# The rows that an expert block computes, cut from three steps of rank to four (128, 112, 104, then 96 from rank 22)

## The reference, cut to what matters

```python
grp = top-1 of 4 groups; two best of the 8 experts in that group     # 32 experts, 1536*2 = 3072 rows
for each expert e, for its own rows xb:                              # xb: tokens that chose e
    h = silu(xb @ w1[e]) * (xb @ w3[e])      # w1, w3: 1024 x 512
    y = h @ w2[e]                            # w2: 512 x 1024
out[token] += gate * y
```

```
144 130 120 117 | 109 108 107 107 107 101 100 100 99 98 | 97 96 96 95 94 92 91 90 | 90 88 88 85 84 78 78 68 59 56
```

## Time and profile before

| | us |
|---|---|
| median of the runs | 1596.06 |
| lowest, highest | 1595.56, 1600.31 |
| the profiled execution | 1602.02 |
| its span, first to last instruction | 1600.4 |
| TensorE busy in the span | 1491.9 (93%) |
| VectorE, ScalarE, GpSimd busy | 524.3, 394.0, 185.2 |
| mean granted TensorE clock | 0.969 of full speed |

### The profile page before, as it was taken

One profiled execution on the slowest core, in us unless ns is written; L12 is line 12 of the kernel. 1 busy time (PEld: TensorE's weight loads), 2 busy tenths in 40 slices (PEclk: granted clock), 3 DMA queues, 4 the chain that ended last, 5 costly groups with the idle time before them and its releaser, 6 DMA issues.

```text
span 1600.4 us, 32656 instructions
## 1 busy us (share of the span) xinstructions
PE 1491.9 (93%) x13884; PEld 948.3 (59%) x13884; DVE 524.3 (33%) x1085; ACT 394.0 (25%) x577; POOL 185.2 (12%) x244
## 2 busy tenths in 40 slices
PE   7999999999999997999893899999999999999990
PEld 3444445555555554545451778777777777777750
DVE  3860035535536545454458201111111111111114
ACT  4120044454446434222440100000000000000004
POOL 2011000110010010011101111111111111111110
PEclk9999999999999998999995899999999999999995
DMA  6132132233123314435582949999999999999968
GB/s 231 40 105 86 66 138 73 73 106 110 63 98 102 118 68 142 160 138 204 201 288 101 361 148 320 360 359 355 357 356 353 357 367 361 367 364 363 365 199 328
DMA packets 75254, 350.07 MB, mean 219 GB/s; under 512 B 9704, under 2 KB 22504, under 8 KB 62752
## 3 DMA queue, kind: packets, MB, share of 16 engines
q1 hardware_dynamic: 56624, 288.31, 48.7%
q0 software_dynamic: 17968, 58.97, 12.4%
q10 hardware_dynamic: 576, 1.59, 0.3%
HBM read 285.69 MB, written 63.14 MB: 218 GB/s over the span
## 4 chain that ended last, share of the span: by engine, by line
PE 52%; DVE 3%; DMA 2%; ACT 2%; issue 2%; DVEq 0%; SPq 0%; POOLq 0%; ACTq 0%
PE bank L1947 24%; PE bank L1965 13%; PE bank L1762 7%; PE bank L1835 2%; PE bank L1920 2%; DMA wup<-w 1%; PE bank L1853 1%; ACT junk L1077 1%; PE bank L1847 1%; PE bank L1705 0%; PE bank L1980 0%; DVE wide L1359 0%; DMA x_dram<-mid,sidx 0%; DVE early L1505 0%; PE bank L1714 0%
## 5 line engine op out<-in xcount | busy, mean ns | idle before, releaser
L1613 PE MATMUL bank<-wide,mid 128*128 128x512 f32 x960 | 422.0, 594 | 1.1 <-issue 1.1
L1947 PEld LDWEIGHTS bank<-xgT,wup 128*64 128x64 f32 (+1 forms) x7680 | 396.2, 141 | 29.6 <-issue 23.7
L1947 PE MATMUL bank<-xgT,wup 128*64 128x104 f32 (+3 forms) x7680 | 403.1, 258 | 5.9 <-issue 3.4
L1613 PEld LDWEIGHTS bank<-wide,mid 128*128 128x128 f32 x960 | 179.4, 190 | 213.5 <-issue 212.8
L1965 PE MATMUL bank<-wide,hidT 128*128 128x512 f32 x512 | 225.6, 593 | 1.6 <-DVE mid L1546 1.6
L1965 PEld LDWEIGHTS bank<-wide,hidT 128*128 128x128 f32 x512 | 94.8, 190 | 109.5 <-issue 107.1
L1537 DVE TENSOR_TENSOR hidT<-sil,bank 128x512 f32<-128x512 f32 x30 | 20.6, 688 | 348.8 <-PE bank L1947 298.2
L1762 PE MATMUL bank<-early,mid 128*128 128x512 f32 x288 | 129.2, 603 | 2.5 <-issue 2.5
L804 POOL DMA_INDIRECT x_dram<-mid,sidx x32 | 50.2, 1568 | 535.1 <-DVE gidx L1523 484.3
L1060 ACT ACTIVATE sil<-bank 128x512 f32<-128x512 f32 x30 | 17.9, 597 | 381.5 <-PE bank L1947 381.5
L1546 DVE TENSOR_SCALAR mid<-bank,gate_of 128x512 f32<-128x512 f32 x64 | 48.0, 751 | 192.8 <-PE bank L1965 192.8
(11 more groups left out here) (250 smaller groups left out, 1254.9 us busy)
## 6 DMA issues: line engine op xcount, KB each, us to landing
wup<-w SPq DMA_DIRECT2D x64, 2048.0 KB, 16.1
wide<-w SPq DMA_DIRECT2D x32, 2048.0 KB, 10.1
u_dram<-ustage POOLq DMA_DIRECT2D x60, 256.0 KB, 2.3
rin<-u_dram SPq DMA_DIRECT2D x60, 256.0 KB, 4.4
mid<-w_in SPq DMA_DIRECT2D x23, 512.0 KB, 3.6
wide<-x_t SPq DMA_DIRECT2D x12, 512.0 KB, 11.5
mix_dram<-mixst POOLq DMA_DIRECT2D x24, 256.0 KB, 2.7
mid<-x_all SPq DMA_DIRECT2D x12, 512.0 KB, 5.5
```

What stands on the lines that cost most here:

```text
L1613: last = pe.matmul(PROJ[u % 3][:, :], wsec[:, slot, k, :], nT[:, k, g * GT:(g + 1) * GT], start=(k == 0), stop=(k == KT - 1))
L1947: last = pe.matmul(target[c0:c0 + wide_tile, at:at + rows], weights[:, s, k, f * P + c0:f * P + c0 + wide_tile], xgT[:, k, 0:rows], start= ...
```

## The change

The number of rows drops in one step more: 112 from rank 4, 104 from rank 14 (16 before), 96 from rank 22 (new). `CAPACITY` feeds everything that has a width: the loops of `blocks_loop` become 4 to 14, 14 to 22, 22 to 30 and 30 to 32, and the matmuls, transposes, gathers and adds take their rows from it. The VectorE lines that work out `cap` from `rank` are written for any number of steps: four instructions of 32 columns in place of three. The bound on overflow blocks is worked out more tightly; it is 30 before and after, so no tensor of the routing changes its width.

```diff
-CAPACITY = ((0, 128), (4, 112), (16, 104))
+CAPACITY = ((0, 128), (4, 112), (14, 104), (22, 96))
+FEWER = 8
 MAIN_BLOCKS = NE
 SIX = 6
-MAX_OVER = -(-(2 * T // (CAPACITY[-1][1] + 1)) // SIX) * SIX
+LEAST, LESS = CAPACITY[-1][1] + 1, CAPACITY[-2][1] + 1
+LATE = min(NE, 2 * T // LEAST) - CAPACITY[-1][0]
+MAX_OVER = -(-(LATE + (2 * T - LATE * LEAST) // LESS) // SIX) * SIX
...
-        cap_step = sb(blockwise, "cap_step", [P, len(CAPACITY) - 1, NE])
+        cap_step = sb(blockwise, "cap_step", [P, NE])
...
-            for i, (first, rows) in enumerate(CAPACITY[1:]):
-                link(dve.tensor_scalar(cap_step[:, i, :], rank[:, :], float(first), float(rows - CAPACITY[i][1]),
-                                       ALU.is_ge, ALU.mult))
-            link(dve.scalar_tensor_tensor(out=cap[:, :], in0=cap_step[:, 0, :], scalar=float(CAPACITY[0][1]),
-                                          in1=cap_step[:, 1, :], op0=ALU.add, op1=ALU.add))
+            steps = [(first, (CAPACITY[i][1] - rows) // FEWER) for i, (first, rows) in enumerate(CAPACITY[1:])]
+            assert all(n == 1 for _, n in steps[1:])
+            link(dve.tensor_scalar(cap_step[:, :], rank[:, :], float(steps[0][0]), float(steps[0][1]),
+                                   ALU.is_ge, ALU.mult))
+            for first, _ in steps[1:]:
+                link(dve.scalar_tensor_tensor(out=cap_step[:, :], in0=rank[:, :], scalar=float(first),
+                                              in1=cap_step[:, :], op0=ALU.is_ge, op1=ALU.add))
+            link(dve.tensor_scalar(cap[:, :], cap_step[:, :], -float(FEWER), float(CAPACITY[0][1]),
+                                   ALU.mult, ALU.add))
```

## The result

The changed kernel took 1602.73 us (median of 18 runs, 1599.02 to 1607.37) against 1599.17 us (18 runs, 1595.56 to 1600.83) for the kernel before: a ratio of 1.0021, 95% interval 1.0014 to 1.0029. That is 0.2% slower, where 0.5% faster was forecast, and it lies outside the range. A difference this small is under the 0.3% that the prediction called telling; with 18 runs each, its interval excludes no change all the same. Of the 14.5 us between 1588.2 and 1602.73, 3.1 are the kernel before itself: the forecast started from 1596.06, the median of three runs, and the median of 18 is 1599.17. The profiled execution took 1604.1 us, with a span of 1602.3.

The account below looks back on a forecast made before the run. TensorE was taken to bind to block 15 or so, the stream of weights and rows from 17; 7.2 (stream) + 0.9 (last step) - 0.2 (`cap` chain) = 7.9 us off 1596.06 gave 1588.2 us, range 1583.5 to 1593.5.

Parts of the forecast that it names:

- The reading of the bound: Expert stage: TensorE binds to block 15 or so, the stream of weights and rows from 17 on.
- no floor from weight loads: Up products: 96 rows take 10.7 us; rival that weight loads hold them at 11.56 us: 1589.1 us, chance 0.02.
- The landing of w1: Weight loads: w1 still lands 18 to 19 us after issue; near 15 would mean TensorE decides.
- The waits for weights: Between steps of the expert stage: waits for w1 begin about block 16.
- The stream's price for a 96-row step: Gather and add both with 96 rows: the stream needs 19.24 us a step, 19.94 less 0.70.
- Its two parts: Stream saving per 96-row step: 0.27 us for eight rows less moved, 0.43 us for leaving 104-row transfers.
- the awkwardness of 104: Indirect gathers and adds: 104 rows make more small packets and slow the stream, taken at 0.43 us a step.
- The gain of 7.2 us between the starts of step 14 and 31: Expert stage, stream decides: 328.0 us in place of 335.2, a gain of 7.2 us.
- The last step: Behind the last w3 only TensorE counts: block 31 gives 0.9 us.
- the one on the loops: One more boundary between loops of different width, on four engines: cost between 0 and 1.3 us, taken as 0.
- The slower rival I named: An expert over its new cap runs a 33rd block of 128 rows, 21.9 us: 1610.1 us, chance 0.03.
- the first weight wait: Expert stage: waits for w1 were to begin about block 16, the 4 us to spare being used up earlier.

Follow-up runs that it names:

- the kernel with even transfers: Kernel before, TensorE at 104 rows from block 16 as before, but gathers and adds of these blocks moving 112 rows: 1596.51 us, ratio 0.9976 to before.
- the one with the moved code: Changed kernel with 128 long-fulfilled waits put in TensorE's queue ahead of the wait for the picks: 1598.41 us, ratio 0.9984 to before.
- the early product: Changed kernel with block 31's down product ahead of the overflow loops where no overflow block is in use: 1589.92 us, ratio 0.9937 to before.
- the one jump: Changed kernel with one more condition around TensorE's overflow loops, left in one jump instead of five rounds: 1591.85 us, ratio 0.9940 to before.
- the run with one loop more: Kernel before with its loop of blocks 16 to 30 cut in two at block 22, widths as before: 1606.04 us, ratio 1.0038.
- the kernel with four widths: Kernel before with 112 rows, 104 from rank 10, 96 from 16, block 31's down product ahead of the overflow loops, even transfers: 1583.97 us, ratio 0.9892.

## Why the prediction was wrong

**What held.** The reading of the bound held. Up products with 96 rows were forecast at 10.7 us and are 10.71 to 10.78: no floor from weight loads. The landing of w1 stays at a median of 17.9 us from step 23 on, and no overflow block ran. The waits for weights came later than forecast, not about block 16 but ahead of block 20 (start, us, what, and in brackets the wait before it):

```profile
1311.12 11.63 PE L1954 MATMUL bank<-xgT,wup 128*64 128x104 f32 x256 [0.77 <-DMA wup<-w]
```

The kernel before, too, has its first wait between steps ahead of block 19 (the 1.02 us at 1293.54 in the earlier trace rows). The stream's price for a 96-row step was put at 19.24 us; eight steps from 23 to 30 took 152.3, 19.0 each. Its two parts held too. A step's packets under 512 B went back from 123 to about 80; the DMA view of step 26 of the changed kernel, without its last 0.4 us, has 77:

```profile
DMA packets 631, 6.72 MB, mean 361 GB/s; under 512 B 77, under 2 KB 77, under 8 KB 269
```

GpSimd's issue of the add went from 1616 ns to 1439, in the view of its line (min/median/max):

```profile
L807 POOL DMA_INDIRECT x_dram<-mid,sidx x7: 1439/1439/1457, 1390.5 to 1505.4; - x7
```

That the awkwardness of 104 costs the stream, taken at 0.43 us a step, is shown by the kernel with even transfers: its step of 19.32 us has 0.33 us less than the 19.65 that went by before, with 8 rows more to move at 0.27 us. That is at least 0.6 us, since TensorE sets the step there: the same side and a little larger. The rule of the Trainium skill that was cited for it, 13 engines for 104 rows ("DMA: Bandwidth & Descriptors"), agrees with this in its consequence, with an estimate of 0.73 us a step in the prediction; how the rows lie on the engines no trace shows.

**The gain of 7.2 us between the starts of step 14 and 31** measured 5.5. The missing 1.7 is about what TensorE waited, with no transfer named, in the first pass through the new loops:

```profile
1212.36 5.32 PE bank L1954 x114
1217.68 0.16 issue
1217.83 5.93 PE bank L1954 x128
1223.76 0.64 issue
1224.40 0.93 PE bank L1954 x14
...
1359.65 1.08 issue
```

These stand inside an up product and not at the start of a matrix, so they aren't waits for w1 or w3, and a q8 packet comes 1 to 3 us ahead of each (in the half microseconds from 1215.0, 1222.0 and 1358.0). Nine of the twelve profiles have a wait in the second block of a loop's first pass with just 14 matmuls of the up products to go, of 0.1 to 1.3 us; the one with the moved code has none there. That they are instruction waits is argued from that, not tried by itself. With the early product, where the waits in step 15 come to 0.2 us, the same stretch took 1519.66 - 1191.75 = 327.9 us; forecast were 328.0.

**The last step** was to bring 0.9 us by block 31. Its up product was 0.85 us shorter, but the transposes lost 1.0, so the term came out at nothing.

**The step that failed** is the one on the loops: "There is one boundary between loops of different width more ... Bounds 0 and 1.3 us; I take 0". I looked for the cost of a longer text at the boundary that was added. It came up behind the last main block, at the overflow loops, which the change doesn't touch: 8.5 us in the profile, 13 us between the medians of the changed kernel and of the one with the early product, 2 of which the kernel before has as well. The bound of 1.3 us was taken from the boundaries between main loops; the nearest row for this jump was the 1.6 us between the last two `down` products in the kernel before, and I gave it no term. With 8.5 us for it, from the profile, the sum comes out 0.6 us slower, and with the 11 us that the one jump brought back 3.1; measured were 3.6 between the medians. The fetch of instructions has a line in the page's DMA part, and I gave it neither a term nor a rival. The slower rival I named, an overflow block, didn't come.

Stated as sizes: without the jump the forecast holds. The kernel with the early product is 10.1 us under before by its ratio; less the 2 us that this edit is worth by itself, the change brings some 8 us, against 7.9 forecast. That the two agree so closely is in part luck, since the term of the last step and the time of the first weight wait were off.

**What stays open.** Why in some executions of one and the same program the wait is there and in others not (two bundles in the run with one loop more) wasn't settled. That the wait is a fetch of instructions rests on what the edits of the program's text did and on the times of the packets; no row names it. Nor was TensorE's exact count of blocks of code ahead of each jump worked out.

## What to carry to other kernels

Count the program's text as a resource: each further loop body moves everything behind it, and a loop whose conditions are all false isn't free when it jumps over its body once a round. Leave unlikely code in one jump and put the work of the usual case ahead of it; here that turned a change from 0.2% slower to 0.6% faster. And try to round the rows of indirect transfers to a multiple that measures well (96 or 112 here, not 104), even where less is computed; it took 4 us off the kernel before and nothing clear off the changed kernel, whose narrow blocks have even transfers already.

## What the runs showed of the hardware that I had not expected

- TensorE stood still for 8.3 us in the changed kernel with all data there, between two products with five rounds of a loop of false conditions between them; with one condition around the loop it didn't stand still at all, and the kernel was 11 us faster.
- The same program text moved by 128 instructions was 4 us faster by the medians.
- The still stretch cost the clock as well: 0.60 and then 0.50 of full speed granted, and 16 matmuls of 512 columns took 8.92 us instead of 7.14. In the kernel with four widths the clock was at 0.50 after only 2.3 us without a matmul, and an up product took 12.44 us instead of 10.71.
- Gathers and adds of 104 rows gave about 45 packets under 512 B more in a step than those of 112, and slowed the weights beside them: 365 GB/s against 373 with 112 rows moved.
